# Level products of the chunk inverses: both directions in one 64x64 matrix, chains by chunk halves

## The reference, cut to what matters

```python
def step(S, inp):                      # one token, one head: S is 64x64
    r_t, w_t, k_t, v_t, a_t, b_t = inp
    sa = jnp.einsum('zbhvk,zbhk->zbhv', S, a_t)
    S = S * w_t[..., None, :] + sa[..., :, None] * b_t[..., None, :] + v_t[..., :, None] * k_t[..., None, :]
    return S, jnp.einsum('zbhvk,zbhk->zbhv', S, r_t)
...
_, ys = lax.scan(step, jnp.zeros((2, B, H, N, N), f32), xs)    # z = 0 forward, z = 1 backward
y = ys[0] + ys[1][:, ::-1]
```

## Time and profile before

| | us |
|---|---|
| median of 3 runs | 1302.03 |
| lowest and highest run | 1299.57 and 1304.67 |
| span of the profiled execution | 1299.2 |
| scan, tiles 0 to 7 in that execution | 843.4 to 1058.4, that is 215.0 |
| one tile in the middle (tile 5) | 26.86 |

### The profile page before, as it was taken

The page is one execution under the profiler, slowest core; times in us unless marked ns, Lnnn a source line. Parts: engine busy times, 40 slices in busy tenths (PEclk is TensorE's granted clock), DMA queues, the critical chain, the costliest instruction groups (busy, mean ns, idle before and its releaser), DMA issues.

```text
span 1299.2 us, 30257 instructions
## 1 busy us (share of the span) xinstructions
PE 1245.1 (96%) x12608; PEld 1127.5 (87%) x12608; DVE 929.6 (72%) x1340; ACT 646.1 (50%) x1045; POOL 431.6 (33%) x222
## 2 busy tenths in 40 slices
PE   7999999999999999999999699899999998999998
PEld 5799999877889999889999699789999887889998
DVE  7677667786877665776677797697777656866664
ACT  5444455553544455645444466743434333655543
POOL 1244432321034444133444100173344512233442
PEclk9999999999999999999999899999999999999999
DMA  8354554422444455645455444110000014545443
GB/s 345 124 179 183 193 194 161 180 98 98 151 177 177 180 188 194 220 169 189 175 180 187 150 171 162 50 52 4 4 4 4 3 52 163 192 180 192 179 177 115
DMA packets 18668, 188.18 MB, mean 145 GB/s; under 512 B 2065, under 2 KB 2577, under 8 KB 3601
## 3 DMA queue, kind: packets, MB, share of 16 engines
q1 hardware_dynamic: 18576, 186.84, 39.4%
HBM read 185.78 MB, written 1.05 MB: 144 GB/s over the span
## 4 chain that ended last, share of the span: by engine, by line
PE 74%; DVE 16%; ACT 7%; issue 2%; DMA 0%; SPq 0%; ACTq 0%; DVEq 0%
PE gu_bank L264 20%; PE gu_bank L266 10%; PE bank L1416 7%; PE bank L243 6%; PE bank L244 6%; PE bank L245 6%; PE gu_bank L1435 5%; DVE WL L198 4%; PE gu_bank L243 3%; ACT WH L186 3%; PE gu_bank L245 2%; PE gu_bank L244 2%; DVE work L512 2%; PE gu_bank L1416 2%; DVE HX L390 1%
## 5 line engine op out<-in xcount | busy, mean ns | idle before, releaser
L207 POOL TENSOR_TENSOR WL<-raw,WH 128x1024 fp32r<-128x1024 f32 x96 | 328.7, 3424 | 602.4 <-ACT WH L192 580.9
L264 PE MATMUL gu_bank<-HX,WH 128*128 128x512 f32 x1408 | 505.6, 401 | 11.1 <-DVE WL L198 8.3
L266 PE MATMUL gu_bank<-HX,WL 128*128 128x256 f32 x1408 | 396.7, 282 | 0.0
L198 DVE TENSOR_TENSOR WL<-raw,WH 128x2048 fp32r<-128x2048 f32 (+1 forms) x114 | 246.5, 2162 | 129.3 <-ACT WH L186 129.3
L264 PEld LDWEIGHTS gu_bank<-HX,WH 128*128 128x128 f32 x1408 | 266.2, 189 | 75.7 <-issue 9.9
L266 PEld LDWEIGHTS gu_bank<-HX,WL 128*128 128x128 f32 x1408 | 267.6, 190 | 0.1
L186 ACT ACTIVATE WH<-raw 128x2048 fp32r<-128x2048 f32 (+1 forms) x114 | 204.6, 1795 | 22.9 <-PE gu_bank L245 13.5
L243 PE MATMUL bank<-PH,WH 128*128 128x256 f32 (+1 forms) x720 | 201.7, 284 | 1.0 <-ACT arena L1973 0.9
L244 PE MATMUL bank<-PL,WH 128*128 128x256 f32 (+1 forms) x720 | 201.6, 283 | 0.0
L245 PE MATMUL bank<-PH,WL 128*128 128x256 f32 (+1 forms) x720 | 201.5, 283 | 0.0
L445 ACT ACTIVATE work<-work 128x256 f32<-128x256 f32 x88 | 36.8, 418 | 258.8 <-DVE work L512 258.8
(11 more groups left out here) (310 smaller groups left out, 1949.4 us busy)
## 6 DMA issues: line engine op xcount, KB each, us to landing
raw<-stream_in SPq DMA_DIRECT2D x114, 1536.0 KB, 6.6
cst<-const_in SPq DMA_DIRECT2D x1, 1568.0 KB, 16.9
X<-xT_in SPq DMA_DIRECT2D x1, 1024.0 KB, 5.2
raw<-stream_in SPq DMA_DIRECT2D x1, 1024.0 KB, 7.2
arena<-hconst_in SPq DMA_DIRECT2D x2, 512.0 KB, 10.6
out<-X SPq DMA_DIRECT2D x4, 256.0 KB, 2.3
arena<-hconst_in SPq DMA_DIRECT2D x1, 768.0 KB, 13.7
arena<-fw_in SPq DMA_DIRECT2D x1, 512.0 KB, 8.0
```

The lines of the kernel that those rows point to most:

```text
L198: nc.vector.tensor_tensor(WL[:, slot, :cut], raw[:, slot, :cut], WH[:, slot, :cut].bitcast(fp32), ALU.subtract).then_inc(lo_ready, 1)
L207: (eng or nc.gpsimd).tensor_tensor(WL[:, slot, cut:end], raw[:, slot, cut:end], WH[:, slot, cut:end].bitcast(fp32), ALU.subtract).then_inc ...
L264: nc.tensor.matmul(out[:, :], WH[:, slot, w:w + P], HX[:, x, :, :].rearrange("p i t -> p (i t)"), start=k == 0, stop=False)
L266: return nc.tensor.matmul(out[:, L:2 * L], WL[:, slot, w:w + P], HH[:, x, :], start=False, stop=k == CT - 1)
```

## The change

**Layout.** The two chains are no longer the two directions but the chunk halves: chain j has chunks 2j and 2j+1, each in both directions. T1 of a chain is one stretch with the two directions 3*64 elements apart. ZBANK and DBANK hold a chain's four units (two directions, two chunks).

**One matrix for both directions.** At level n the late side of z = 0 is the early side of z = 1. XL(n) of a chunk is now one 64x64 matrix: the columns of the second kind of block come from A of one direction, the others from A of the other, with disjoint columns. T0 is made the same way, by transposing the early columns of both directions, interleaved block by block (`early_cols`). A product then takes as moving operand the 32 late columns of direction 0 and the 32 of direction 1 together (`late_cols`), 64 columns in all; what belongs to the wrong direction meets only zeros. So a chain has 2 chunks x 2 heads products of 64 columns in `zee` and in `update` (8 records each) where it had 4 chunks x 2 heads products of 32 columns (16 records each).

**What else has another size.** XL(n) is 128x128 for a chain instead of 128x256, read with an interleaved pattern of runs of b elements. The transpose into T0 is 128x128 instead of 128x256, also with interleaved reading. ScalarE's copy into ZB stays 128x128 and becomes contiguous; VectorE's adds stay 128x128; the masks, the identity and the copies of A stay 128x256. ZB is one buffer for all levels, and the four GpSimd memsets that cleared it before the scan go. In `zee(n,0)` `pe_r` comes as two products for each of the two chunks, where it was one for each of four; the order of everything else is as before.

```diff
-        def side_heads(dst, at, n, w, x):
+        def both_dirs(dst, n, w, x):
             for h in range(2):
                 r = slice(HD * h, HD * h + HD)
-                out_ = dst[r, at:at + CH // 2].rearrange("p (k b) -> p k b", b=LEVELS[n])
-                last = nc.tensor.matmul(out_, w[r], x[r], start=True, stop=True)
+                last = nc.tensor.matmul(dst[r], w[r], x[r], start=True, stop=True)
             return last
+        def late_cols(a, n, q, c=None):
+            b, at, w = LEVELS[n], q * TS + (c or 0) * CH, 2 * CH if c is None else CH
+            a = a[:, at + b:at + b + 2 * (ZS - b)].rearrange("p (z x) -> p z x", z=2)[:, :, 0:w]
+            return a.rearrange("p z (k h b) -> p z k h b", h=2, b=b)[:, :, :, 0, :]
+        def early_cols(a, n, at, w, zs):
+            b = LEVELS[n]
+            a = a[:, at:at + 2 * (zs + b)].rearrange("p (z x) -> p z x", z=2)[:, :, 0:w]
+            return a.rearrange("p z (k h b) -> p k z h b", h=2, b=b)[:, :, :, 0, :]
...
-            def zee(n, z, c):
-                return side_heads(ZBANK[z], c * CH // 2, n, XL[n][:, z, c], side(TQ[:, z, 1, c], n, late(z)))
+            def of_chunk(a, n, c):
+                return a.rearrange("p (z c s) -> p c z s", z=2, c=2)[:, c].rearrange("p z (k b) -> p z k b", b=LEVELS[n])
+            def zee(n, j, c):
+                return both_dirs(of_chunk(ZBANK[j][:, 0:P], n, c), n, XL[n][:, j, c], late_cols(T1, n, j, c))
...
-                for c in range(NCH):
-                    zb = ZB[n][:, z, c]
-                    zb = side(zb, n, late(z)) if n < len(LEVELS) - 1 else zb.rearrange("p (k b) -> p k b", k=1)
-                    last = side_heads(DBANK[z], P + c * CH // 2, n, TQ[:, z, 0, c], zb)
+                for c in range(2):
+                    zb = ZB[:, z, :, c, :].rearrange("p z (k b) -> p z k b", b=LEVELS[n])
+                    last = both_dirs(of_chunk(DBANK[z][:, P:L], n, c), n, T0[:, z, c], zb)
...
-                for c in range(NCH):
+                for c in range(2):
                     last = zee(n, 0, c)
                     if step and n:
-                        r = pe_r(pe, q, n, c // 2, c % 2 == 1)
+                        for value in (False, True):
+                            r = pe_r(pe, q, n, c, value)
...
-                for c in range(NCH):
+                for c in range(2):
                     last = zee(n, 1, c)
                     if n in (1, 2):
-                        tr = pe_tr(pe, p, n, (2 * c, 2 * c + 1))
+                        tr = pe_tr(pe, p, n, range(4 * c, 4 * c + 4))
...
-            def turned(z, ready):
+            def turned(n, j, ready):
                 dve.wait_ge(t_ready, ready)
-                nc.vector.transpose(TQ[:, z, 0].rearrange("p c s -> p (c s)"), TQ[:, z, 1].rearrange("p c s -> p (c s)"))\
-                    .then_inc(t0_ready, 1)
+                mine = early_cols(T1, n, j * TS, 2 * CH, ZS)
+                nc.vector.transpose(T0[:, j].rearrange("p c s -> p (c s)"), mine).then_inc(t0_ready, 1)
...
-                    nc.gpsimd.tensor_tensor(XL[n][:, z], ABD[:, z], mask64("level", (z * len(LEVELS) + n) * CH), ALU.mult)\
-                        .then_inc(xl_ready, 1)
+                    mine = early_cols(ABD, n, z * L, 2 * CH, 2 * CH)
+                    turns = lambda a: a.rearrange("p (k z b) -> p k z b", z=2, b=LEVELS[n])
+                    nc.gpsimd.tensor_tensor(turns(XL[n][:, z].rearrange("p c s -> p (c s)")), mine,
+                                            turns(ccols("level", 2 * CH, 2 * n * CH)), ALU.mult).then_inc(xl_ready, 1)
```

More of the change, by code:

```diff
@@ L75 @@
 _cn = [("ones", P), ("ident", P), ("istack", CH), ("blockones", P), ("sel", CT * 16), ("selt", CT * P), ("perm", P),
-       ("first", 2 * CH), ("first_incl", 2 * P), ("strict_incl", 2 * P), ("level", len(LEVELS) * 2 * CH), ("reset", L)]
+       ("first", 2 * CH), ("first_incl", 4 * CH), ("strict_incl", 2 * P), ("level", len(LEVELS) * 2 * CH), ("reset", L)]
 CC = {}
@@ L1534, in pe_tile @@
                 pe.wait_ge(t_ready, 12 * t)
-            for z in range(2):
-                for c in range(NCH):
-                    u = z * NCH + c
-                    last = heads(DBANK[z], at64(c, P), beta[:, u], both(p, u))
+            for j in range(2):
+                for n in range(4):
+                    u = n // 2 * NCH + 2 * j + n % 2
+                    last = heads(DBANK[j], at64(n, P), beta[:, u], both(p, u))
                 last.then_inc(aq_done, 1)
-            for z in range(2):
-                for c in range(NCH):
-                    u = z * NCH + c
-                    last = heads(ZBANK[z], at64(c), AR[p][:, u, 0], beta[:, u])
+            for j in range(2):
+                for n in range(4):
+                    u = n // 2 * NCH + 2 * j + n % 2
+                    last = heads(ZBANK[j], at64(n), AR[p][:, u, 0], beta[:, u])
                 last.then_inc(a_done, 1)
@@ L1673, in act_tile @@
             A, cp, q = nc.scalar.activation, ACT.Copy, 1 - p
-            for z in range(2):
-                act.wait_ge(a_done, 2 * t + z + 1)
-                A(ABD[:, z], z_bank(z), cp).then_inc(abd_ready, 1)
+            for j in range(2):
+                act.wait_ge(a_done, 2 * t + j + 1)
+                A(ABD[:, j * L:(j + 1) * L], ZBANK[j][:, 0:L], cp).then_inc(abd_ready, 1)
             if ahead:
@@ L1704, in act_tile @@
                     act_high(act, 0)
-            for z in range(2):
-                act.wait_ge(t_ready, 12 * t + 10 + z - 1)
-                keep = side(TQ[:, z, 1].rearrange("p c s -> p (c s)"), len(LEVELS) - 1, 1 - late(z))
-                A(side(QF[:, z * NCH:(z + 1) * NCH, :].rearrange("p c s -> p (c s)"), len(LEVELS) - 1, 1 - late(z)), keep, cp)\
-                    .then_inc(qf_ready, 1)
+            for j in range(2):
+                act.wait_ge(t_ready, 12 * t + 10 + j - 1)
+                keep = [early_cols(a, len(LEVELS) - 1, j * TS, 2 * CH, ZS) for a in (QF, T1)]
+                A(keep[0], keep[1], cp).then_inc(qf_ready, 1)
             if t:
@@ L2455, in _ @@
             pool.wait_ge(blocks_done, 3 * S_O)
-            for zb in ZB[:-1]:
-                last = nc.gpsimd.memset(zb, 0.0)
-            last.then_inc(zb_clear, 1)
             def pool_step(t, p, c, a):
@@ L2516, in _consts @@
             m = (t // (2 * b) == s // (2 * b)) & ((t // b > s // b) if z == 0 else (t // b < s // b))
-            put("level", np.tile(m * 1.0, (2, 1)), (z * len(LEVELS) + n) * CH)
+            side = np.arange(CH) // b % 2 == z
+            cols = np.flatnonzero(side)
+            for copy in range(2):
+                consts[:, CC["level"] + (2 * n + copy) * CH + cols] = np.tile(m * 1.0, (2, 1))[:, cols]
     put("reset", np.tile((np.arange(L) % CH != 0) * 1.0, (P, 1)))
```

90 lines of the change are left out of this document (44 added, 46 removed).

## The result

The changed kernel takes 1286.2 us (median of four runs, 1283.7 to 1288.4) beside 1302.5 us (1299.6 to 1304.7) for the kernel before: a ratio of 0.9865, with a 95% interval of 0.9835 to 0.9895. That is 16.3 us less. A later measurement (five runs of the changed kernel, nine of the one before) gave 1283.6 against 1304.7, a ratio of 0.9838 (0.9814 to 0.9862). The forecast was 1285.9.

A forecast was written before the change was run, and what follows sets the result against it. TensorE looks busy, but round trips and VectorE end many steps. Tiles 1 to 6 give 12.0 us, tile 0 1.3, tile 7 2.8: 1302.0 - 16.1 = 1285.9 us; forecast 1279 to 1292 (74%), 8 in 10 1277 to 1295.

The forecast's parts named there:

- The price of a record: Level products, line 1435: 29.2 ns each at 32 or 64 columns, so at most 4.67 us per tile.
- Rival 3: Level products: one of 64 columns takes two slots of 29.2 ns, leaving 1300 us; chance 6%.
- The step from `pe_u` to `pe_u`: Middle tile walked level by level: 1.98 us kept up to `pe_u` of level 3, 0.33 of it at the start.
- `update(n,0)` gives nothing: Levels 1 to 3: the round trip over VectorE's copy of U hides the shorter products; kept 0, 0.70 us a tile.
- A wait for the state: Between levels, TensorE waits for ScalarE's state copy before `zee`: slack of 0.1 goes, a wait of 0.15 us comes.
- VectorE's four products ahead of the copy of R(3): Before `pe_u` of level 3: TensorE's records count for nothing, the shorter transpose for 0.13 us.
- GpSimd at the end of the tile: Middle tile's end: line 1775 would run into GpSimd's line 1909, giving back 0.43 us.
- Tiles 1 and 2: Counted among the middle tiles, each keeping 2.0 us of 4.67; tile 1's half-clock stretch left where it is.
- TensorE as the bound: Whole scan: waits find other cover, gaining up to 37.4 us, 1264.6; chance 4%.
- rival 2: Transposes: interleaved reading makes short ones as long as the old, losing 0.66 us a tile, 1291; chance 8%.
- rival 4: TensorE's clock drops with more waiting, one stretch a tile at about 1.5 us, 1296; chance 3%.
- rival 5: GpSimd's XL operations of level 0 get longer in runs of 2 elements, ten us slower, 1312; chance 5%.

The follow-up runs named there:

- with GpSimd out of the way: Changed kernel with a buffer of its own for GpSimd's sum, so GpSimd no longer waits for the bonus product: middle tile 24.31 us, total 1280.3.
- with VectorE earlier: Changed kernel with VectorE's copy of y of the tile before moved to ScalarE: middle tile 24.73 us, total 1286.5.
- The three experiments on the kernel before: Kernel before with level products, transposes of levels 1 to 4, or both, over two of four chunks only: middle tile 25.31, 26.73, 25.02 us.
- the version with all four edits: Changed kernel with GpSimd's sum buffer, copy of R between VectorE's products, y's copy on ScalarE, `zee(n,0)` before the state wait: 1275.4 us, ratio 0.9785.

## Why the prediction was right, point by point

**The price of a record: right.** There are 160 records a tile, and eight of them (981.30) are followed by the next group at 981.53, 0.23 us later: 29 ns each; a product of 64 columns costs what one of 32 cost, and splitting it costs the gain back (26.73). Rival 3, two slots a product, is out. The Trainium skill, page "PSUM — Partial Sum Buffer", section "Specifications (TRN2)", says that any non-contiguous access pattern slows matmuls significantly; here the products write two runs of 32 elements with a gap, and no slowing shows at 29 ns a record. The measurement decides. The Trainium skill, page "TensorEngine Tiling (Array Packing)", section "Instruction Overhead", says that each product has an overhead of some 60 cycles, so that one with a single column takes as long as one with 60; the trace agrees as far as it goes, with 29 ns for 32 and for 64 columns.

**The step from `pe_u` to `pe_u`: right, but for the first.** Position of `pe_u` in tile 5, counted from the tile's first mask, and its gain:

| `pe_u` of | before | after | gain | forecast |
|---|---|---|---|---|
| level 0 | 5.07 | 4.60 | 0.47 | 0.33 |
| level 1 | 10.25 | 9.02 | 1.23 | 1.08 |
| level 2 | 15.04 | 13.29 | 1.75 | 1.62 |
| level 3 | 19.56 | 17.47 | 2.09 | 1.98 |
| next tile | 26.86 | 24.73 | 2.13 | 2.0 |

The differences from row to row were forecast as 0.75, 0.54, 0.36 and 0.02 and are 0.76, 0.52, 0.34 and 0.04. Only the start of the tile was mis-sized, 0.47 instead of 0.33. The cause is how VectorE's slack was read. In the kernel before:

```profile
979.70 1.27 DVE L1826 TENSOR_TENSOR scan<-bank,cst 128x512 f32<-128x512 f32 x2
```

The masks' record ends at 980.97 and the copy of R starts at 981.08, which I took as a slack of 0.1. But two operations that follow without a wait overlap in the records: in the changed kernel the masks end at 975.05 and the copy starts at 974.98. The slack was 0.11 + 0.07 = 0.18, and with the two transposes' 0.27 it covers 0.45 of TensorE's 0.47.

**`update(n,0)` gives nothing: right.** In level 1 `pe_u` to `pe_s` takes 0.84 us with 8 records in between (979.73 to 980.57), where it took 0.79 with 16. The slots of the last of them end at 980.01 + 8 x 0.029 = 980.24, and `pe_s` follows 0.33 later, where 0.37 was forecast; the profile's own column says 0.16, since records last longer than their slots.

**A wait for the state: there, and smaller.** 0.09 us instead of 0.15. Moving `zee` ahead of it showed that it is worth next to nothing by itself, because level 3 takes it back.

**VectorE's four products ahead of the copy of R(3): right.** The forecast said that TensorE's records count for nothing there; the wait grew from 0.51 to 0.72, and taking it away gave 0.53 a tile.

**GpSimd at the end of the tile: right in kind, 0.09 too large, and another term made up for it.** Line 1775, now 1781, takes 1.15 us for two where it took 0.81: 0.34 given back, not 0.43. They met as forecast: GpSimd's operation ends 0.53 us after line 1781 starts (992.49 and 991.96), where 0.56 was worked out (998.25 and 997.69). The first of the two also ended as forecast, 0.28 after GpSimd's (992.77 and 992.49), where 0.29 was read from tile 0. What was off is what it was compared with: I took 0.42 for the first operation alone, but in the kernel before it took 0.48 (1000.03 to 1000.51), since it already met the end of line 1909 there. 0.811 - 0.475 is the 0.34. Against that, the 0.11 for TensorE starting behind VectorE's bound came to 0.02: the next tile's first product started 0.17 us after VectorE's last add ended (1002.08 and 1001.91) and now starts 0.15 after it (994.32 and 994.17). So two errors of like size cancel, and the last row of the table above has 0.04 more than the one before it, where 0.02 was forecast. The edits at this place, with GpSimd out of the way (0.42 gained) and with VectorE earlier (0 gained), show that the cost is real and what it hangs on.

**Tiles 1 and 2: 3.1 and 2.6 instead of 2.0, the step that failed most.** I gave all middle tiles the working of tile 5 and left the shorter XL operations of GpSimd at nothing, with "the prefix sums no longer meet an XL operation" only in the spread. Tile 2 of the kernel before:

```profile
901.27 2.79 POOL L1919 TENSOR_TENSOR scan<-raw,cst 128x256 f32<-128x256 f32 x4
...
903.30 1.30 DVE L1730 TENSOR_TENSOR_SCAN arena<-cst,arena 128x256 f32<-128x256 f32 x1
```

Tile 5 of the same kernel:

```profile
982.44 3.19 POOL L1919 TENSOR_TENSOR scan<-raw,cst 128x256 f32<-128x256 f32 x4
...
984.46 0.65 DVE L1730 TENSOR_TENSOR_SCAN arena<-cst,arena 128x256 f32<-128x256 f32 x1
```

And tile 2 of the changed kernel:

```profile
900.99 1.69 POOL L1937 TENSOR_TENSOR scan<-raw,cst 128x128 f32<-128x128 f32 x4
...
903.59 0.65 DVE L1736 TENSOR_TENSOR_SCAN arena<-cst,arena 128x256 f32<-128x256 f32 x1
```

An XL operation takes 0.45 us instead of 0.72, so the ten of tile 2 end 7.3 us into the tile instead of 10.0 (902.68 - 895.40 and 904.05 - 894.07), and VectorE's prefix sum no longer meets them: 0.65 us instead of 1.30. But a meeting as such isn't what made tile 2 longer. In tile 5 the prefix sum meets the last XL operation too, and there GpSimd is the one held: the four take 3.19 us instead of 2.79 (the last one 1.12 instead of 0.72) and the prefix sum takes 0.65. Tiles 3, 4 and 6 are like tile 5. In tile 2 VectorE was held, for 0.65 us: its copy of R of step 1 starts 10.39 us after the first mask, 9.73 in tile 5, and 0.51 of that is left at the tile's end. The two records of tile 2 start within 0.02 us of each other (903.30 and 903.32), so which engine is held hangs on very little, and the traces don't show what decides it. The three experiments on the kernel before, whose XL operations are as wide as ever, have prefix sums of 0.65 to 0.75 us in tile 2 and no longer tile there. So the 0.5 us by which tile 2 gained more than tile 5 are a held VectorE that the change happened to remove, and a forecast taken from tile 5 could not have them.

Tile 1 is less clear. Its prefix sum took 0.81 us beside the last XL operation and takes 0.65 now, which is 0.16. At its end TensorE, with products of the next projection, was the later of the two before: VectorE's last add ends at 893.19 and the next tile's first product starts at 894.07. So TensorE's shorter records count there, where in tile 5 VectorE set the end. These are readings of two traces, no run isolates them, and tile 1 has a stretch at half clock that doesn't always lie at the same place: in the seven executions of the changed kernel and its edits with 160 records tile 1 takes 25.3 to 27.3 us from mask to mask, without following the edits. Why it gained 1.1 more than forecast stays open.

Tile 0 gave 0.36 more than forecast. Its ten transposes saved 10 x 0.134 = 1.34, and VectorE's operation of line 1737 (now 1743), which had lain beside GpSimd's sum (line 1925, 854.11 to 854.82), fell from 0.80 to 0.38 us. This too is read from the two traces and not isolated.

**Tile 7: 2.64 instead of 2.8.** The terms in the prediction add up to 2.88. The difference was not followed up.

**The four memsets.** They don't end before the first product, as the prediction says: they run from 842.34 to 844.25, and the first product starts at 843.38. Nothing in the table of tiles points to a price of theirs.

**The total: two errors against each other.** The scan gave 18.6 instead of 16.1. Of the 2.5, tiles 1 and 2 are 1.7, tile 0 is 0.4, tiles 3 to 6 are 0.6, and tile 7 takes 0.2 back. The medians differ by 16.3 (the interval runs from 13.7 to 21.5), less than the scan. The profiled execution began its scan 6.1 later, with 20.4 us more at half clock ahead of it; the second measurement, 21.1 us, lies on the other side. So the closeness of 1286.2 to 1285.9 is in part luck, and says less than the tile lengths do: a middle tile 24.73 against 24.9, tile 0 18.75 against 19.1, tile 7 26.74 against 26.6.

**The rivals.** TensorE as the bound (22.2 a tile) is out: more than half of its 4.67 us a tile is not kept. Long transposes (rival 2) are out: line 1826 takes 0.31 us at 128x128 with interleaved reading, and the 0.13 that I took from other operations is what it saves. Lower clock by more waiting (rival 4): the middle tiles have 1.00, tile 1 has 0.94 in both. GpSimd slower in short runs (rival 5): 0.45 us, shorter than before.

## What to carry to other kernels

For small float32 products count instructions, not columns: two products of 32 columns with the same stationary matrix can be laid side by side for the price of one (no run here goes beyond 64 columns in these products). Then walk the chain of waits and ask at each one what is late next; here 160 x 29 ns = 4.67 us a tile became 2.13, and the working of one tile's steps said so beforehand. Before VectorE's work is moved or shortened ahead of an operation with two SBUF inputs, look at what GpSimd does at that moment: 0.39 us taken off VectorE was worth nothing, because VectorE then only ran into GpSimd's operation earlier, and it did so again in the version with all four edits. And apply that look to every tile that differs from the one that was walked.

## What the runs showed of the hardware that was not expected

- The same unchanged code ahead of the scan ends between 843 and 852 us from execution to execution, in step with how long TensorE was at half of its clock there (17.1 to 44.4 us), while a middle tile of the scan repeats to a few hundredths of a microsecond, with three exceptions in twelve executions. One span by itself can't tell an edit of less than some 5 us; the usual tile length can tell one of a few hundredths.
- VectorE beside GpSimd was stopped, not slowed: the operation of line 1775 (1781, 1785) that met GpSimd's ended 0.28 us after it, whether it had started 1.21 (tile 0 of the kernel before), 0.87 (the copy of y on ScalarE) or 0.53 us (the changed kernel) before GpSimd's end. It can fall on either engine: where the prefix sum met an XL operation, VectorE's took 1.30 us instead of 0.65 in tile 2, and GpSimd's took 1.12 to 1.15 instead of 0.72 in tiles 3 to 6.
- A transpose of 128x256 takes 0.445 us and one of 128x128 0.311 us, with interleaved reading, so halving the size saves 0.134; GpSimd's product fell from 0.72 to 0.45 with runs of b elements.
- A product that writes two separate runs of 32 elements in PSUM takes its 29 ns slot as one with a single run does.
